# Where the last down piece of an expert stands among the up pieces after it, and where the residual rows are added

## The reference

```
for e in range(N_EXPERTS):                       # 16
    gate, up = jnp.split(hf @ wu[e], 2, axis=-1) # wu[e]: 2048 x 1024
    out = out + combine[:, e:e + 1] * ((jax.nn.silu(gate) * up) @ wd[e])  # wd[e]: 512 x 2048
x = x + out, then a final rmsnorm of x
```

## Time and profile before

| what | value |
|---|---|
| median of 3 runs | 1818.7 us (1818.69 to 1822.36) |
| profiled execution | 1819.89 us, its span 1817.9 us |
| PE busy | 1711.7 us, 94% of the span |
| DVE, ACT busy | 62%, 57% |
| granted TensorE clock, mean of the span | 0.985 of full |
| last 12 of the 40 slices | 350 to 378 GB/s, but for the last |

### The profile page before, as it was taken

The page is one execution under the profiler, slowest core; times in us unless marked ns, Lnnn a source line. Parts: engine busy times, 40 slices in busy tenths (PEclk is TensorE's granted clock), DMA queues, the critical chain, the costliest instruction groups (busy, mean ns, idle before and its releaser), DMA issues. The chain is left out here.

```text
span 1817.9 us, 28754 instructions
## 1 busy us (share of the span) xinstructions
PE 1711.7 (94%) x10780; PEld 1489.3 (82%) x10780; DVE 1128.9 (62%) x1422; ACT 1031.3 (57%) x1507; POOL 128.5 (7%) x176
## 2 busy tenths in 40 slices
PE   5999989999999999999899999999999899899897
PEld 5999989999998898889899999997665565566554
DVE  5888883444444444444444446457878877887885
ACT  6666663333344434444333335557788788888775
POOL 2545530000000000000000000000000000000000
PEclk9999999999999999999899999999999999999998
DMA  8556655657646645653856575445899999999994
GB/s 199 148 152 163 167 150 139 164 159 189 185 124 167 170 129 140 175 142 108 194 154 172 151 194 136 135 160 203 324 378 363 350 361 370 366 369 368 367 376 200
DMA packets 418894, 393.55 MB, mean 216 GB/s; under 512 B 19169, under 2 KB 376897, under 8 KB 409665
## 3 DMA queue, kind: packets, MB, share of 16 engines
q1 hardware_dynamic: 407152, 383.04, 66.2%
q10 hardware_dynamic: 10432, 4.79, 1.0%
q0 software_dynamic: 1232, 4.72, 0.9%
HBM read 385.38 MB, written 11.08 MB: 218 GB/s over the span
## 5 line engine op out<-in xcount | busy, mean ns | idle before, releaser
L702 ACT ACTIVATE wH<-ring 128x1024 fp32r<-128x1024 f32 x320 | 335.8, 1058 | 535.4 <-PE bank L1156 474.4
L1605 DVE TENSOR_TENSOR wL<-ring,wH 128x1024 fp32r<-128x1024 f32 x320 | 388.0, 1230 | 374.8 <-ACT wH L702 366.8
L1154 PE MATMUL bank<-hH,wH 128*128 128x288 f32 x1792 | 536.5, 299 | 5.7 <-ACTq L764 2.7
L1155 PE MATMUL bank<-hL,wH 128*128 128x288 f32 x1792 | 530.5, 296 | 0.0
L1156 PE MATMUL bank<-hH,wL 128*128 128x288 f32 x1792 | 530.0, 296 | 0.0
L1820 DVE SCALAR_TENSOR_TENSOR sL<-raw,prm,sH 128x1024 fp32r<-128x1024 f32 x256 | 317.6, 1280 | 64.8 <-ACT sH L910 63.5
L1154 PEld LDWEIGHTS bank<-hH,wH 128*128 128x128 f32 x1792 | 339.0, 189 | 12.9 <-issue 7.0
L1155 PEld LDWEIGHTS bank<-hL,wH 128*128 128x128 f32 x1792 | 338.8, 189 | 0.4
L1156 PEld LDWEIGHTS bank<-hH,wL 128*128 128x128 f32 x1792 | 338.6, 189 | 0.0
L910 ACT ACTIVATE sH<-raw,prm 128x1024 fp32r<-128x1024 f32 x256 | 284.0, 1153 | 57.4 <-PE bank L1392 25.6
L1390 PE MATMUL bank<-sH,hgs 128*128 128x512 f32 x512 | 176.4, 426 | 21.8 <-DVE sL L1820 18.8
(11 more groups left out here) (324 smaller groups left out, 2108.0 us busy)
## 6 DMA issues: line engine op xcount, KB each, us to landing
raw<-in_expert_w_up SPq DMA_DIRECT2D x128, 1024.0 KB, 7.8
ring<-in_w_in SPq DMA_DIRECT2D x112, 1024.0 KB, 7.2
raw<-in_expert_w_down SPq DMA_DIRECT2D x64, 1024.0 KB, 7.4
ring<-in_w_pb SPq DMA_DIRECT2D x16, 1024.0 KB, 9.1
ring<-in_w_pa SPq DMA_DIRECT2D x16, 1024.0 KB, 8.9
ring<-in_w_o SPq DMA_DIRECT2D x16, 1024.0 KB, 5.9
cK<-in_cache_k SPq DMA_DIRECT2D x16, 256.0 KB, 2.8
cV<-in_cache_v SPq DMA_DIRECT2D x16, 256.0 KB, 3.3
```

Of the source, the lines that this page charges most:

```text
L702: a.activation(wH[2 * (slot % 2) + half][:, :, :], ring[slot][:, 8 * half:8 * half + 8, :], ACT.Copy).then_inc(hi_ready, 1)
L1154: pe.matmul(dst, hi, rH[:, k, :], start=(k == 0), stop=False)
L1155: pe.matmul(dst, hi, rL[:, k, :], start=False, stop=False)
L1605: v.tensor_tensor(lo[:, :, :], ring[slot][:, 8 * half:8 * half + 8, :], hi[:, :, :].bitcast(F32), ALU.subtract).then_inc(lo_ready, 1)
```

## The change

In fourteen strings (of those that the stream uses, all but the first) the carried down piece, which stood behind the second up piece of the next expert, stands behind the first. It is always D3 of the expert before. The number of splits and their order on ACT and DVE are the same; what moves there is which slot each split reads, and the work that is placed by `DONE_AT`, which is now one up piece earlier.

The residual rows are no longer added behind the wait for atL at the group's first down piece, but right behind the remap, which is one up piece earlier; the wait for `scaled_ready` moves with them.

```
-PLANS = ["UU-UUDUDUDUU", "UU-UDUUDUUDU", "UU-UDUUDUUUD", "UU-UDUUDUUDU"] * NG
-PLANS[0], PLANS[NE - 2] = "UUUUDUDUDUU", "UU-UDUUUDUU"
+PLANS = ["U-UUUDUDUDUU", "U-UUDUUDUUDU", "U-UUDUUDUUUD", "U-UUDUUDUUDU"] * NG
+PLANS[0], PLANS[NE - 2] = "UUUUDUDUDUU", "U-UUDUUUDUU"
...
                         remap(x, x // EPG % 2, x % EPG, pair[x % 2][0])
+                        if x % EPG == 0:
+                            pe.wait_ge(es_ready, x // EPG + 1)
+                            need(pe, scaled_ready, 4 * (x // EPG))
+                            residual(xsH, True, False)
+                            residual(xsL, False, False)
...
                 if t == DOWN_AT[e]:
                     pe.wait_ge(atL_ready, e + 1)
-                    if j == 0:
-                        if g == 0:
-                            pe.wait_ge(es_ready, 1)
-                        need(pe, scaled_ready, 4 * g)
-                        residual(xsH, True, False)
-                        residual(xsL, False, False)
```

## The result

The changed kernel is slower: median 1837.24 us (1833.28 to 1838.74, 4 runs) against 1820.28 us (1818.69 to 1822.36, 4 runs), a ratio of 1.0089 with a 95% interval of 1.0073 to 1.0104. The forecast was 1825.5 us, with a range from 1811 to 1833. The sign was right, the size was not: +17 us where +6.8 were worked out. The profiled execution took 1836.34 us, its span 1834.4 us.

The account below looks back on a forecast made before the run. PE's waits in time order were taken to bound the expert stage, neither PE nor DMA being full. Terms 6.0 + 1.0 - 1.5 + 0 + 2.1 - 0.8 = +6.8 us gave 1825.5 us as median, range 1811 to 1833.

Parts of the forecast that it names:

- the rival that the DMA engines bound the stage: Expert stage: same bytes take the same time, so PE's waits only move; 1818.7 us, no change, chance 0.18.
- The first step: D3 before U1's second half on PE: 1.19 us wait covered, 0.5 gained; behind 2, 6, 10 -1.5 us together.
- S: Start of the first split of U1; the prediction timed U2, actHL and 4D0 from it. S' is after the change.
- The second step: U1 fetched in D3's place lands later; U2 2.0 us later behind 5, 9, 13: +6.0 us, bounds 3.6 and 9.0.
- the place behind 1: Second step behind expert 1: slot wait without a table load, U2 1.0 us later, bounds 0 and 1.2.
- Behind 14: Later landing would cost 1.6 us, D3's earlier free slot offsets up to 2: taken as 0, bounds -0.5 and 1.6.
- Behind 3, 7 and 11 no wait is there to gain, and PE reaches the remap when it did: 0.: Places where D2 comes late and covers the wait before U1's second half: 0 us; late fifth-piece fetch counted at group starts.
- The third step: Group starts: atL wait goes, 2.45 us gained at equal S, but S' later: +0.7 each, +2.1 for three.
- At the first group: No old sums to read; the residual goes into the gap before U3: -0.8 us.
- I take the clock as costing what it did.: Assumption on PE's granted clock in the sum: no added cost from stretches at 1.2 GHz.
- The third rival: Longer PE waits at the remap make the clock fall more often, 2 to 3 us each: 1833 us, chance 0.10.
- The rival that the landing does not decide: U1 in its slot in time everywhere, so gains hold: 12.2 us, 1806.5 us; half of it some 1813; chance 0.20.

Follow-up runs that it names:

- fetch_act5: fetch_kept with the split of the activations (actHL on ACT and DVE) taken one place earlier among the splits; 1800.71 us, 0.9895 of the kernel before.
- fetch_kept: The changed kernel's order on all engines, but SP fetches U1 ahead of D3 as before, slots following; 1810.24 us, 0.9945 of the kernel before.
- filler: The changed kernel with matmuls without use ahead of the remaps behind experts 1, 5, 9, 13 and 14; 1831.3 us, 1.0066 of the kernel before.
- res_only: The kernel before with only the residual rows moved behind the remap, old strings kept; 1821.68 us, 1.001 of the kernel before.

## Why the prediction was right in sign and wrong in size

**What bounds the kernel.** Right. PE's waits in time order decide; the rival that the DMA engines bound the stage is out, since with the same bytes fetch_act5 has a stage of 539.5 us against 556.0. That is also less than the 562 us that the rival needed.

**The first step (D3 ahead of U1 on PE).** Right, and measured where S did not move: -1.6 for the three places worked out at -1.5. Kernel after behind expert 6 (answer to the earlier trace rows); S is 1482.85 and U2 comes at S + 9.2, the bound itself:

```profile
1482.85 1.15 ACT L910 ACTIVATE sH<-raw,prm 128x1024 fp32r<-128x1024 f32 x1 [3.06 <-PE bank L1392]
...
1491.63 0.62 PE L1464 MATMUL bank<-RT,actHL 128*128 128x96 f32 x4 [0.77 <-DVE actHL L2018]
1492.08 0.70 PE L1390 MATMUL bank<-sH,hgs 128*128 128x512 f32 x2
```

**The second step (U1 fetched one place later).** Right in mechanism, as fetch_kept shows, and right in the choice within its bounds behind 5: U2 1.8 us later nominally, 2.0 worked out. The waits at the remap were 3.6 us where 2 to 3 were foreseen. The term was mis-sized by what follows such a wait behind 5 and 9: 6.8 us at 1.2 GHz, which cost 1.9 and 2.1 us more. Behind 13 the kernel before has such a stretch too, and the place cost 2.2 us, about as worked out. The three places cost 9.9 us and not 6.0, and the place behind 1 3.0 and not 1.0 (there the landing alone was 1.9). Behind 14 the shift at U2 is 0.7 us, within its bounds, and the low stretch at 1784 makes it 1.9, past the bound of 1.6. In filler, with the clock kept up, the places cost 1.4, 1.6 and 0.7 behind 5, 9 and 13, 1.3 behind 1 and nothing behind 14: the late fetch by itself costs about what was worked out, or less, but for 0.3 us behind 1.

**"Behind 3, 7 and 11 no wait is there to gain, and PE reaches the remap when it did: 0."** This is the step that failed, by 8.5 us, the largest miss: 5.7 us of longer waits for hgs and 2.8 us in the clock that follows. PE's way to the remap was looked at, but not ACT's list: the last hgs copy stands behind U1's splits there, and PE's wait for it was already in the trace of before, 2.2 us in 3 places, small and not followed up. The prediction treated U1's late landing there only as a slot that comes free later.

**The third step (group starts).** Worked out +2.1, measured +1.1. 4D0 started at S' + 15.6 (1424.09 - 1408.51) for the 15.75 worked out, and PE's wait went from atL to the multiplications of the old sums, 1.8 us each, as foreseen; S' came 3.2 us later than S, 3.1 foreseen. The rest is a low stretch of the kernel before in the second group's start, which the change doesn't have. The third group has a low stretch in neither kernel and cost 1.8 us, past the bound of 1.5. Of this, 8D0 is 0.4 us late, where 0.7 was worked out; the rest comes with a new wait of 1.01 us for the split of 8D1 (the same at 4D1), which the prediction did not have. At the first group 0D0 gained 1.4 for 0.8. What the step claimed of the residual by itself, 2.45 us at equal S, was never realized in any run: without early D3 the old sums take atL's place (res_only), and with it nothing measurable is won.

**"I take the clock as costing what it did."** Wrong. The third rival had the mechanism (1833 us) and got 0.10; in the trace the low stretches went from 23.9 to 37.5 us in the stage, and filler wins 5.3 us by removing most of those at the remaps. The rival that the landing does not decide was what fetch_kept then built: 1806.5 worked out for it, 1810.2 measured.

**Median and trace.** 3.1 us of the stage's 19.5 are hidden in the profiled executions by a faster start, in code that is the same.

## What to carry to other kernels

A list that is order, fetch order and slot order at once can hide a gain: moving a piece on the consumer moved its neighbour's fetch, and that cost 27 us (changed kernel against fetch_kept) where the move alone brings 10; ask for each moved item what now comes later in the fetch queue, and separate the two orders before the idea is given up. When a piece lands later, follow everything that stands behind it on each in-order engine, the small waits (2.2 us here) above all, for they are where the delay comes out. After each removed wait name the next one: actHL one place earlier was worth nothing before D3 moved, and 6.2 us in the stage and 9.5 in the median after. And count a wait that moves together with the clock that may fall in it.

## What the runs showed of the hardware that was not expected

The time up to the expert stage, the same instructions in all thirteen kernels, took 1244.3 to 1249.2 us in the profiled executions, with 13.7, 20.5 or 23.9 us of it at the lower clock. So a difference of less than 5 us between two profiles is read from the stage and not from the span.

Matmuls without use made the kernel faster (5.3 us in the stage): behind 1, 5, 9 and 14 PE stayed at its higher clock. And in short windows the DMA engines moved more than the 405 GB/s of the earlier trace rows, here in fetch_kept, the remap's wait and the low clock after it:

```profile
1446.00:1449.80 3.80, 2.03 (x11) 1.48 (x10) 3.74 (x4) 2.22 (x4) 0.00 (x0) 1.00 1.03 409
1449.80:1453.20 3.40, 3.40 (x9) 2.50 (x9) 2.62 (x4) 2.90 (x5) 0.00 (x0) 0.50 1.01 418
```
